# Second mixer: one tap and the bias of the convolution on ScalarE, the key products on GpSimd

## What is computed

```python
z, xbc, dt_raw, cq, ckv, kr, gates = split_cols(u @ w_in[l], IN_SPLIT_SIZES)

# SSD branch: xbc has 3072 channels, 24 tiles of 128
xbc = silu(causal_depthwise_conv(xbc, conv_w, conv_b))   # 4 taps, y[t] = b + sum_k w[k] x[t-3+k]
xs, bm, cm = split_cols(xbc, (2048, 512, 512))

# MLA branch: 8 heads, 128 + 64 dimensions, kr shared by the heads
k = concatenate([k_nope, broadcast(kr)])
k = rms_norm_2(k, k_norm_g)               # one reciprocal root per head and token
k = concatenate([k[..., :128], apply_rope(k[..., 128:], cos, sin)])
```

## Time and profile before

| what | us |
|---|---|
| median of 3 runs | 3698.76 (3694.76 to 3703.43) |
| profiled execution, first to last instruction | 3618.2 |
| TensorE busy | 3233.4 (89%) |
| VectorE busy | 2382.8 (66%) |
| ScalarE busy | 1604.2 (44%) |
| GpSimd busy | 1238.8 (34%) |

### The profile page before, as it was taken

The page is one execution under the profiler, slowest core; times in us unless marked ns, Lnnn a source line. Parts: engine busy times, 40 slices in busy tenths (PEclk is TensorE's granted clock), DMA queues, the critical chain, the costliest instruction groups (busy, mean ns, idle before and its releaser), DMA issues. The chain is left out here.

```text
span 3618.2 us, 51767 instructions
## 1 busy us (share of the span) xinstructions
PE 3233.4 (89%) x18906; PEld 2536.7 (70%) x18906; DVE 2382.8 (66%) x4616; ACT 1604.2 (44%) x3514; POOL 1238.8 (34%) x1211
## 2 busy tenths in 40 slices
PE   6997888887789898888877999999999999999999
PEld 5895444442278754444423998898899998898899
DVE  7776766666576566666765657767666657767665
ACT  3643333333355433333323444665544545665443
POOL 1306777777712177777775000000000000000000
PEclk8999999999999999999999999999999999999999
DMA  8568999999965499999998453343355553343454
GB/s 302 205 235 345 409 409 409 409 400 371 385 250 190 158 409 409 409 409 409 389 360 332 160 181 137 125 139 135 134 185 183 182 180 136 124 141 130 139 183 162
DMA packets 258297, 937.20 MB, mean 259 GB/s; under 512 B 29312, under 2 KB 30720, under 8 KB 257792
## 3 DMA queue, kind: packets, MB, share of 16 engines
q0 software_dynamic: 161280, 587.27, 41.7%
q1 hardware_dynamic: 96768, 346.62, 27.6%
HBM read 932.73 MB, written 1.05 MB: 258 GB/s over the span
## 5 line engine op out<-in xcount | busy, mean ns | idle before, releaser
L700 PE MATMUL M<-rows,diag 128*128 128x512 f32 x2048 | 988.9, 615 | 242.1 <-DMA rows<-in_expert_v_dram,expert 226.0
L278 DVE TENSOR_TENSOR w_low<-ring,w_high 128x1024 fp32r<-128x1024 f32 x560 | 686.1, 1228 | 413.3 <-ACT w_high L270 410.7
L700 PEld LDWEIGHTS M<-rows,diag 128*128 128x128 f32 x2048 | 363.7, 191 | 821.6 <-DMA rows<-in_expert_v_dram,expert 503.4
L1222 DVE CUSTOM_DVE_ANT_0 rows<-rows,attn 128x1024 f32<-128x1024 f32 x512 | 623.6, 1225 | 473.5 <-DMA rows<-in_expert_u_dram,expert 471.1
L297 PE MATMUL G<-x_high,w_high 128*128 128x256 f32 x2576 | 763.0, 296 | 48.7 <-DVE w_low L278 15.7
L270 ACT ACTIVATE w_high<-ring 128x1024 fp32r<-128x1024 f32 x560 | 588.7, 1054 | 350.3 <-PE G L297 326.1
L300 PE MATMUL G<-x_high,w_low 128*128 128x256 f32 x2576 | 739.7, 287 | 0.0
L299 PE MATMUL G<-x_low,w_high 128*128 128x256 f32 x2448 | 704.5, 288 | 0.0
L422 POOL DMA_INDIRECT rows<-in_expert_u_dram,expert x512 | 550.2, 1075 | 296.0 <-issue 155.4
L422 POOL DMA_INDIRECT rows<-in_expert_v_dram,expert x512 | 555.1, 1084 | 157.4 <-issue 115.5
L297 PEld LDWEIGHTS G<-x_high,w_high 128*128 128x128 f32 x2576 | 506.0, 196 | 62.3 <-issue 37.1
(11 more groups left out here) (361 smaller groups left out, 5055.2 us busy)
## 6 DMA issues: line engine op xcount, KB each, us to landing
ring<-in_stream_dram SPq DMA_DIRECT2D x654, 512.0 KB, 3.4
ada_ring<-in_ada_stream_dram POOLq DMA_DIRECT2D x80, 512.0 KB, 5.0
rows<-in_ada_stream_dram POOLq DMA_DIRECT2D x16, 512.0 KB, 16.2
rows<-in_expert_u_dram,expert POOLq DMA_INDIRECT x512, 11.7
rows<-in_expert_v_dram,expert POOLq DMA_INDIRECT x512, 11.7
const<-in_const_dram SPq DMA_DIRECT2D x1, 1096.5 KB, 11.1
x<-in_x_dram SPq DMA_DIRECT2D x1, 1024.0 KB, 5.5
out_dram<-x SPq DMA_DIRECT2D x8, 128.0 KB, 3.7
```

Source lines behind the costliest of these rows:

```text
L278: dve.tensor_tensor(T["w_low"][:, part, :], T["ring"][:, place.slot(chunk, slots), :], T["w_high"][:, part, :].bitcast(F32), ALU.subtract) ...
L700: mm = pe.matmul(M[:, 2 * t + half, :], T["diag"][:, n % 4, :], T["v_rows"][:, n % SLOTS, half * 512:(half + 1) * 512], start=(h == 0 and ...
L1222: dve.tensor_tensor_reduce(row, row, T["x_tok"][:, t, :], 1.0, 0.0, ALU.mult, ALU.add, T["hid"][:, r, k:k + 1]).then_inc(sem["u_used"], 1)
```

## The change

In the convolution ScalarE, before its copy to cpad, also writes the last tap and the bias from PSUM into the conv buffer: an Identity with scale and bias from columns of parameters. It waits for conv_done of two tiles before, since that buffer alternates. VectorE starts with tap 0 on top of it: three operations instead of four.

For the keys, VectorE keeps only the reciprocal, into one of two buffers (rstd and the last tile of xm), after a wait for GpSimd's work of two heads before. GpSimd multiplies rope_k and the nope tile, both as 128x256. So that a whole tile can be multiplied, the rotated key is kept three times: as it is, and with the upper or the lower 64 rows set to zero by a column of ones and zeros (half_rows). VectorE's wait for its own products after each head goes, and ssd_halves waits for all eight heads at its ninth tile.

```diff
+        def key_unit(h):
+            u = MLA_HEADS + h
+            inverse = T["k_rstd"][h % 2]
+            pool.wait_ge(sem["rstd_ready"], norm_of["unit"] + u + 1)
+            pool.tensor_tensor(T["rope_k"][:, h, :], T["rope_out"][:, h % 2, :], inverse[:, :], ALU.mult)
+            pool.tensor_tensor(T["nope"][:, u, :], T["nope"][:, u, :], inverse[:, :], ALU.mult
+                               ).then_inc(sem["qk_ready"], 1)
+
         before = 0 if opening else KD - 1
         add_up(T["ysq"][:, 0, :], [T["ysq"][:, k, :] for k in range(1, KX)], sem["ysq_ready"], 0,
                sem["sq_added"], before)
+        for h in range(MLA_HEADS):
+            key_unit(h)
...
                 if n >= 2:
                     act.wait_ge(sem["conv_sum"], n - 1)
+                    act.wait_ge(sem["conv_done"], n - 1)
                 if n == 0:
                     act.wait_ge(sem["pads_ready"], 1)
+                act.wait_ge(g_full, g + 1)
+                last = n * CONV + CONV - 1
+                act.activation(T["conv"][:, n % 2, :], G[:, g % GB, 0:S], ACT.Identity,
+                               bias=p2("conv_b")[:, n:n + 1], scale=p2("conv_w")[:, last:last + 1])
                 copy_out(g, T["cpad"][:, n % 2, CONV - 1:])
...
-            link(dve.tensor_scalar(out, pad[:, 0:S], wj[:, 0:1], p2("conv_b")[:, j:j + 1], ALU.mult,
-                                   ALU.add))
-            for tap in range(1, CONV):
+            for tap in range(CONV - 1):
                 ins = dve.scalar_tensor_tensor(out=out, in0=pad[:, tap:tap + S], scalar=wj[:, tap:tap + 1],
                                                in1=out, op0=ALU.mult, op1=ALU.add)
...
-            out = T["rope_q"][:, j, :] if j < PAIRS else T["rope_out"][:, :]
+            out = T["rope_q"][:, j, :] if j < PAIRS else T["rope_out"][:, 2, :]
             link(dve.tensor_tensor(out, T["rope_in"][:, j, :], T["cos2"][:, :], ALU.mult))
             link(dve.tensor_tensor(out, out, T["rope2"][:, :], ALU.add))
+            if j == PAIRS:
+                for n in range(2):
+                    dve.tensor_scalar(T["rope_out"][:, n, :], out, T["half_rows"][:, n:n + 1], None, ALU.mult)
+
+        def half_rows():
+
+            for n in range(2):
+                for half in range(2):
+                    link(dve.memset(T["half_rows"][MLA_ROPE * half:MLA_ROPE * (half + 1), n:n + 1],
+                                    float(n == half)))
...
-            inverse_std(n)
-            rows = slice(MLA_ROPE * (h % 2), MLA_ROPE * (h % 2 + 1))
-            other = slice(MLA_ROPE * (1 - h % 2), MLA_ROPE * (2 - h % 2))
-            dst = T["rope_k"][:, h, :]
-            link(dve.tensor_tensor(dst[rows, :], T["rope_out"][rows, :], rstd[rows, :], ALU.mult))
-            dve.memset(dst[other, :], 0.0)
-            dve.tensor_tensor(T["nope"][:, u, :], T["nope"][:, u, :], rstd[:, :], ALU.mult
-                              ).then_inc(sem["qk_ready"], 1)
-            dve.wait_ge(sem["qk_ready"], h + 1)
+            if h >= 2:
+                dve.wait_ge(sem["qk_ready"], h - 1)
+            inverse_std(n, T["k_rstd"][h % 2])
...
             if k == 0:
                 dve.wait_ge(sem["std_ready"], norm_of["ffn2"])
+            elif k == KD:
+                dve.wait_ge(sem["qk_ready"], MLA_HEADS)
```

More of the change, by code:

```diff
@@ L2136, in conv @@
             wj = p2("conv_w")[:, j * CONV:(j + 1) * CONV]
-            link(dve.tensor_scalar(out, pad[:, 0:S], wj[:, 0:1], p2("conv_b")[:, j:j + 1], ALU.mult,
-                                   ALU.add))
-            for tap in range(1, CONV):
+            for tap in range(CONV - 1):
                 ins = dve.scalar_tensor_tensor(out=out, in0=pad[:, tap:tap + S], scalar=wj[:, tap:tap + 1],
                                                in1=out, op0=ALU.mult, op1=ALU.add)
-                if tap < CONV - 1:
+                if tap < CONV - 2:
                     link(ins)
@@ L2352, in vector @@
                 masks()
+            elif (kind, j) == ("kr", 0):
+                half_rows()
             elif kind == "out":
@@ L2583, in program @@
                 T2["rstd_ssd"] = sb2("rstd_ssd", S)
+                T2["k_rstd"], T2["half_rows"] = (T2["rstd"], T2["xm"][:, KD - 1, :]), T2["c_in"][:, 0:2]
                 for name in ("dt", "acum_n"):
@@ L2602, in program @@
                         T2[name] = part(work, n * (PAIRS + 1) * S, PAIRS + 1, S)
-                    T2["rope_out"] = part(work, 2 * (PAIRS + 1) * S, S)
+                    T2["rope_out"] = part(work, 2 * (PAIRS + 1) * S, 3, S)
                     T2["probs"], T2["probsT"] = part(work, 0, 2, TT, S), part(work, 4 * S, 2, TT, S)
```

## The result

The changed kernel takes 3668.8 us (median of 4 runs, 3666.8 to 3670.6) beside 3698.0 (3694.8 to 3703.4) for the kernel before in the same comparison: a ratio of 0.9919, 95% interval 0.9907 to 0.9931. Two more comparisons gave 0.9925 (0.9913 to 0.9937) and 0.9909 (0.9893 to 0.9925). The forecast was 3678.0: faster by 20.8 us, where it became 28 to 34 by the three ratios. The sign and the mechanisms held, the size did not. One profiled execution of the changed kernel took 16248.6 us where its other runs have a median of 3662.0, and its trace isn't used.

What follows compares the result with a forecast made beforehand. VectorE, 0.25 us late each xs step, bounds the convolution and a dependency loop the key heads. Per layer 3.7 + 1.3 + 5.6 - 0.2 = 10.4 us, two layers 20.8, gives 3678.0 us; range 3668 to 3690.

Steps and rivals of the forecast that it cites:

- Convolution, 3.7 us a layer: Convolution with tap and bias on ScalarE: the stretch falls from 79.02 us to TensorE's own 75.3, gaining 3.7 us.
- the step with a group's products on top: Convolution: TensorE's xs step with a group's products, taken as 3.88 us against 3.10 for one without.
- The stop ahead of the third z tile, 1.3: Start of the z steps: with VectorE up to date, 1.2 us instead of 2.5 to the next projection, gaining 1.3.
- Key heads, 5.6: Key heads: shorter loop gives back 6.2 us of TensorE's stops, less 0.6 for GpSimd getting in ahead of the squares.
- Rotation, 0.2: Key rotation: two masked copies cost nothing to 0.8 us, taken as a loss of 0.2 us a layer.
- the steps behind the heads: ssd_low beside the last head's products: at worst 0.2 us later, behind 6.4 us of value tiles, so no cost.
- rival A: End of the convolution: a shorter stop keeps the clock up, 2.5 us a layer, 5 in all: 3673 us; chance 0.18.
- the second pause: Early z steps: the longer pause, said to hang on decay exponentials after a table load and to stay unchanged.
- 80.6 us around the span: Whole kernel: profiled span 3618.2 us lies 80.6 below the median 3698.8; this difference was added back unchanged.
- B: Key heads: GpSimd's products block VectorE in the loop, gaining 0.4 us at best there: 3688 us; chance 0.13.
- C: Convolution: ScalarE's extra operation delays each copy and TensorE's weights, so part 1 gains nothing: 3688 us; chance 0.07.
- D: Convolution: Identity not loaded with Silu, two table loads of 1.28 us a step, slower: 3760 us; chance 0.03.

## Why the prediction was right in direction and wrong in size

- **Convolution, 3.7 us a layer: 4.1.** From the third bc projection to the transposes after the second z projection it is 74.93 us (2291.13 to 2366.06) where I had summed 75.3. The mechanism is as told: VectorE was 0.25 us late in each xs step, and isn't now. The mis-sized term is the step with a group's products on top, 3.88 by the earlier trace rows; without arrears it is 3.74. Four of them make 0.56 us.
- **The stop ahead of the third z tile, 1.3: 1.3** (2.12 to 0.84).
- **Key heads, 5.6: 5.9.** Seven stops became two, 0.92 and 1.21. One square was blocked, as allowed for: 0.95 us for 0.42, 0.53 of blocking where I took 0.6. Of the 6.2 us that I had without it 0.3 are missing.
- **Rotation, 0.2: 0.1**, and 0.1 more in the steps behind the heads, which I had put at nothing: VectorE's first eight ssd_low rows last 3.85 us instead of 2.77 beside GpSimd's last product.
- **The sum is where it failed.** These terms make 22.2 us for 20.8. The other 6 to 12 us of the 28 to 34 measured are for the most part the clock, and it has no term in the sum; I had made it rival A, 5 us at a chance of 0.18, and argued against it that the second pause stays. That looked only at the one place. What the runs show in its place: 1.4 us behind the stop in one of two layers, 1.2 behind the next in the other, 3.5 in the stretches after the softmax, 6.1 together. Another 1.7 us stand ahead of the convolution in one trace of after and not in the other, so they are chance, and what is left isn't placed. A sum over edited stretches alone was the error: when a stop goes or moves, slow matmuls can go with it, and some of these stand far from it.
- **80.6 us around the span.** 1.8 are; the rest was a faster first block in that execution, as the runs on one of the later chips have it. Which chip that trace is from, no record says. The difference from before to after doesn't hang on it, but I should have asked what the number was.
- **Rivals B, C and D** are out. B: GpSimd's products take 0.97 (once a layer 1.77) and 0.73 to 2.05 us, and VectorE's low halves beside them 1.57 to 1.76 for 1.23, but only one square a layer waits for that. C: ScalarE hides the Identity. D: no table load. That is also what the Trainium skill says (page "ScalarE: Activation LUTs", section "Table sets: the hidden batching unit"), and here the trace bears it out: the one load in these 77 us is the one ahead of the first Silu (2290.71). The lock between VectorE and GpSimd of the Trainium skill's page "SBUF — State Buffer" (section "SBUF: two separate sides") is there too, 0.95 us for a square of 0.42, but counted on the loop it is 0.9 us a layer at most and not 6.

## What to carry to other kernels

When a change takes stops of 1 to 3 us out of the bounding engine, or shifts them, give the clock a term of its own in the sum: here 1.4 to 1.8 us where a stop of over 2 us went or was filled and its slow matmuls with it, nothing where it had none behind it, and a quarter to a half on top of the edited stretches overall. Part of that is luck of timing, since the same stop had a run of slow matmuls behind it in one layer and not in the other. Before an operation is moved to another engine, look at the order in VectorE's queue: VectorE's z product put ahead of its neighbours brought some 10 us more, a third of the whole change, for no work moved. And compare traces between fixed instructions, not by their spans, when parts that no edit touches differ by more than the effect.

## What the runs showed of the hardware that I had not expected

- The slow matmuls need not begin with the stop's end: behind the 3.25 us stop above a few run 0.12 us apart before 16 run 0.21 apart; behind the stop of 2.12 us in the second layer of the kernel before, 13 such matmuls begin at once.
- The same stop of 2.73 us is followed by a granted clock of 0.86, 0.89, 0.93 or 0.96 over 48 us, in executions and layers of one and the same kernel too (after: 0.89 and 0.96; its second trace 0.96 and 0.89). It is 0.86 where the fall of the clock comes within 0.4 us of the restart (13 of 13), and higher where it comes later or not at all (15 of 15).
- Matmuls whose result nobody reads keep the clock at 1.00 through a stop, and are worth it only if they are shorter than the stop. In place they gave 1.5 us in both layers at the 3.25 us stop, and 1.4 in one layer of two at the 2.12 us stop; in the sum nothing was seen with one stop filled, and 6.3 us in the trace with four.
- An Identity with scale and bias columns out of PSUM holds ScalarE for 0.46 us of pitch at 128x256 (0.56 from start to end), not more than from SBUF.
- GpSimd's product of 128x256 takes 0.73 us where VectorE is idle and up to 2.05 beside its operations; both engines get longer, VectorE's low half by 0.35 to 0.55 us.
